# Expert stage: rows gathered by an indirect DMA and transposed, one-hot columns on ScalarE, job order alternated

## The reference, cut to what matters

```
g_sel = argmax(hf @ w_r1 + b_r1)              # one of 4 groups per token
top_p, top_i = top_k(softmax(e_logits of the group), 2)
expert_id = g_sel * 4 + top_i                 # 2 of 16 experts per token
combine = sum(one_hot(expert_id) * g_w * top_p)
hid = silu(hf @ w_gate[e]) * (hf @ w_up[e])   # width 256, per expert e
out = sum over e of (hid * combine[:, e]) @ w_down[e]
x = x + out
```

## Time and profile before

| | us |
|---|---|
| median of 3 runs | 1548.86 (1538.7 to 1549.76) |
| the profiled execution: time | 1550.05 |
| its span (first to last instruction) | 1547.3 |

### The profile page before, as it was taken

How to read it: one execution, slowest core, us unless ns; L and a number is a source line. 1 busy time by engine, 2 the same in 40 slices (tenths; PEclk the granted TensorE clock), 3 DMA queues, 4 the chain that set the end, 5 groups by cost and what they waited for, 6 DMA issues and landing times.

```text
span 1547.3 us, 18980 instructions
## 1 busy us (share of the span) xinstructions
PE 1440.7 (93%) x7049; PEld 1137.5 (74%) x7049; DVE 737.5 (48%) x1502; ACT 718.1 (46%) x1176; POOL 578.9 (37%) x261
## 2 busy tenths in 40 slices
PE   5999888989899998999899999999999888999998
PEld 4787665457777765867778777888887776888886
DVE  2196454444520224247854351233323376777775
ACT  4542325234642546445444755435322435555661
POOL 3265111003253311413322244223543156676762
PEclk9899999889999998999999999999999879999999
DMA  4232111003552211312222122212343036565552
GB/s 149 68 104 78 45 42 36 16 22 109 177 153 82 68 55 42 103 47 69 76 68 62 55 77 82 82 61 89 102 139 99 14 115 199 177 181 186 178 185 89
DMA packets 82003, 146.21 MB, mean 94 GB/s; under 512 B 12382, under 2 KB 14740, under 8 KB 81908
## 3 DMA queue, kind: packets, MB, share of 16 engines
q1 hardware_dynamic: 78288, 140.40, 29.5%
q10 hardware_dynamic: 3332, 4.53, 1.0%
q0 software_dynamic: 288, 0.02, 0.0%
HBM read 140.72 MB, written 4.19 MB: 94 GB/s over the span
## 4 chain that ended last, share of the span: by engine, by line
PE 76%; DVE 14%; ACT 6%; issue 2%; DMA 1%; POOL 0%; SPq 0%; DVEq 0%; ACTq 0%
PE ps L894 17%; PE ps L895 17%; PE ps L896 17%; PE ps L1349 4%; DVE perm L2664 3%; DVE work L2491 2%; PE ps L1421 2%; PE ps L1422 2%; DVE best L2489 2%; PE ps L1033 1%; PE ps L1234 1%; PE ps L1251 1%; PE ps L1207 1%; PE ps L1288 1%; PE ps L1269 1%
## 5 line engine op out<-in xcount | busy, mean ns | idle before, releaser
L841 POOL TENSOR_TENSOR w_lo<-raw,w_hi 128x1024 fp32r<-128x1024 f32 (+2 forms) x190 | 454.3, 2405 | 861.5 <-ACT w_hi L1599 832.5
L1599 ACT ACTIVATE w_hi<-raw 128x1024 fp32r<-128x1024 f32 (+3 forms) x206 | 208.7, 1038 | 121.1 <-PE ps L896 109.6
L894 PE MATMUL ps<-w_hi,act_hi 128*128 128x512 f32 (+1 forms) x560 | 231.7, 414 | 7.5 <-POOL w_lo L841 5.9
L895 PE MATMUL ps<-w_lo,act_hi 128*128 128x512 f32 (+1 forms) x560 | 219.6, 392 | 0.0
L896 PE MATMUL ps<-w_hi,act_lo 128*128 128x512 f32 (+1 forms) x560 | 219.1, 391 | 0.0
L894 PE MATMUL ps<-w_hi,mix_hi 128*128 128x512 f32 x384 | 161.7, 421 | 11.1 <-DVE mix_lo L2225 6.4
L896 PE MATMUL ps<-w_hi,mix_lo 128*128 128x512 f32 x384 | 152.2, 396 | 0.0
L895 PE MATMUL ps<-w_lo,mix_hi 128*128 128x512 f32 x384 | 152.2, 396 | 0.0
L894 PEld LDWEIGHTS ps<-w_hi,act_hi 128*128 128x128 f32 (+1 forms) x560 | 104.6, 187 | 47.8 <-issue 14.2
L896 PEld LDWEIGHTS ps<-w_hi,act_lo 128*128 128x128 f32 (+1 forms) x560 | 104.3, 186 | 25.1
L895 PEld LDWEIGHTS ps<-w_lo,act_hi 128*128 128x128 f32 (+1 forms) x560 | 104.7, 187 | 23.7 <-issue 1.7
(11 more groups left out here) (467 smaller groups left out, 2646.9 us busy)
## 6 DMA issues: line engine op xcount, KB each, us to landing
raw<-in_w_in SPq DMA_DIRECT2D x92, 512.0 KB, 3.6
raw<-in_w_gate SPq DMA_DIRECT2D x64, 256.0 KB, 2.9
raw<-in_w_up SPq DMA_DIRECT2D x64, 256.0 KB, 3.3
raw<-in_w_down SPq DMA_DIRECT2D x32, 512.0 KB, 4.1
raw<-in_w_out SPq DMA_DIRECT2D x16, 512.0 KB, 3.7
raw<-in_w_mem_kv SPq DMA_DIRECT2D x16, 512.0 KB, 4.6
raw<-in_w_o_gla SPq DMA_DIRECT2D x8, 512.0 KB, 3.8
raw<-in_w_o_dsa SPq DMA_DIRECT2D x8, 512.0 KB, 3.8
```

The costliest lines, as they stand in the source:

```text
L841: pool.tensor_tensor(lo[:, 0:a], raw_slot(g)[:, 0:a], hi[:, 0:a].bitcast(F32), ALU.subtract).then_inc(*POOL.done(("w_lo", g)))
L894: pe.matmul(dst, l_hi, r_hi, start=start, stop=False, skip_group_check=skip)
L895: pe.matmul(dst, l_hi, r_lo, start=False, stop=False, skip_group_check=skip)
L1599: nc.scalar.activation(split_slot(g)[0][:, 0:a], raw_slot(g)[:, 0:a], ACTF.Copy).then_inc(*ACT.done(("w_hi", g)))
```

## The change

- From pair 1 on the rows of a pair come by two indirect DMAs on GpSimd, each 128 rows of 4 KB, from x stored in `out` in device memory. SyncE stores x there ahead of the fifth expert unit (four stores of 512 KB, counted by `spilled`). The token numbers ride in `combine_r` as two more columns, so that `combine_s` (now 36 columns) yields them; VectorE copies them to `ids`.
- `row_turn` (`xturn`) transposes the gathered rows on TensorE, 4 chunks of 128 features a job, 4 jobs a pair; ScalarE and VectorE evict 128 columns at a time.
- `perm` of pairs 1 to 7 is made by ScalarE: Abs(iota - so), then Relu(1 - that). Pair 0 stays on VectorE.
- Four slots for `y_hi` and `y_lo`; unsort jobs of a pair are spread over the next even and odd visit, four each; the odd visit alternates them with the row jobs; `combine_s` and the gather stand at the end of even visits (visit 0: after `up`).
- VectorE loads the branch register after its part of `turn` in visit 3 (the fourth).

```diff
@@ make_order @@
         pair = e // 2
-        gather = [("resort", pair + 1, 0), ("resort", pair + 1, 1), ("combine_s", pair + 1), ("resort", pair + 1, 2), ("resort", pair + 1, 3)]
+        gather = [("combine_s", pair + 1), ("gather", pair + 1)] if pair + 1 < N_EXP // 2 else []
+        rows = [("xturn", pair + 1, j, i) for j in range(2) for i in range(2)]
         turns = [("permT", pair + 1, j) for j in range(2)]
-        if e < 2:
-            jobs = [gather, turns][e]
+        back = [("unsort", e - 2 - e % 2, 2, t, n) for t in ((2, 3) if e % 2 else (0, 1)) for n in range(2)] if e >= 2 else []
+        wanted = [("weights", E_UNITS * e + 9 + i) for i in range(4)]
+        order += [("up", e), wanted[0]]
+        if e % 2 == 0 and 2 <= e < N_EXP - 2:
+            order += [("perm", pair + 1, 2, 3)]
+        if e == 0:
+            order += gather + [wanted[1], ("turn", e), wanted[2], wanted[3]]
+        elif e % 2 == 0:
+            order += back[:2] + [wanted[1], ("turn", e)] + back[2:] + [wanted[2], wanted[3]]
         elif e == N_EXP - 1:
-            jobs = [("unsort", e - 1, 1, t, n) for n in range(2) for t in range(NT)]
-        elif e % 2:
-            jobs = gather + turns
+            one = [("unsort", e - 1, 1, t, n) for n in range(2) for t in range(NT)]
+            order += back + [wanted[1]] + one[:2] + [("turn", e), wanted[2], wanted[3]] + one[2:]
         else:
-            jobs = [("unsort", e - 2, 2, t, n) for t in range(NT) for n in range(2)]
-        at = (len(jobs) + 1) // 2
-        wanted = [("weights", E_UNITS * e + 9 + i) for i in range(4)]
-        order += [("up", e), wanted[0]] + jobs[:at - 1] + [wanted[1]] + jobs[at - 1:at] + [("turn", e), wanted[2]]
-        order += jobs[at:] + [wanted[3], ("down", e), ("weights", E_UNITS * e + 14)]
-        if e and e < N_EXP - 3:
-            order += [("perm", (e + 3) // 2, *((0, 1) if e % 2 else (2, 3)))]
+            order += back[:2] + rows[:1] + [wanted[1], ("turn", e)] + back[2:3] + rows[1:2] + back[3:] + [wanted[2]] + rows[2:3]
+            order += turns[:1] + rows[3:] + [wanted[3]] + turns[1:]
+        order += [("down", e)]
+        if e % 2 == 0 and e:
+            order += gather
+        order += [("weights", E_UNITS * e + 14)]
+        if e % 2 and e < N_EXP - 3:
+            order += [("perm", pair + 2, 0, 1)]
@@ tiles @@
-        y_hi = sb("y_hi", [P, 2, D], SC + 44, F32R)
-        y_lo = sb("y_lo", [P, 2, D], SC + 52, F32R)
+        y_hi = sb("y_hi", [P, 4, D], SC, F32R)
+        y_lo = sb("y_lo", [P, 4, D], SC + 44, F32R)
+        xg = sb("xg", [P, 2, 2, D], SC + 16)
@@ SyncE, at the loads of weights @@
+                if g == expert_unit + RAW_SLOTS:
+                    for t in range(NT):
+                        sp.wait_ge(*DVE.after("x", "w_out21", t))
+                        sp.dma_start(out[0, P * t:P * (t + 1), :], x1[:, t, :]).then_inc(spilled, 16)
@@ GpSimd @@
+                elif step == "gather":
+                    pair = a[0]
+                    pool.wait_ge(spilled, 16 * NT)
+                    pool.wait_ge(*DVE.after("ids", pair))
+                    if pair < 3:
+                        pool.wait_ge(*PE.after("resorted", 0, 3))
+                    else:
+                        pool.wait_ge(*PE.after("xturned", pair - 2, 1, 1))
+                    for j in range(2):
+                        pool.indirect_dma_start(xg[:, pair % 2, j, :], None, out[0, :, :],
+                                                bass.IndirectOffsetOnAxis(ids[:, pair % 2, j:j + 1], 0)).then_inc(g_in[pair % 2], 16)
@@ TensorE @@
+            def row_turn(pair, j, i):
+                bank = job_bank["xturn", pair, j, i]
+                claim(bank, (DVE, ("s_lo", 2 * pair + j, 4 * i + 3)))
+                pe.wait_ge(g_in[pair % 2], 32 * ((pair + 1) // 2))
+                for k in range(4):
+                    tr = pe.transpose(ps[:, bank, P * k:P * k + P], xg[:, pair % 2, j, paired_rows(4 * i + k)], ident[:, :])
+                tr.then_inc(*PE.done(("xturned", pair, j, i)))
@@ ScalarE @@
+            def one_hot(pair, *tiles):
+                if pair == 0:
+                    return
...
+                for t in tiles:
+                    for j in range(2):
+                        e = 2 * pair + j
+                        op = nc.scalar.activation(perm[:, t, P * j:P * j + P], iota[:, :], ACTF.Abs, bias=so_minus[:, t, e:e + 1])
+                    op.then_inc(*ACT.done(("perm_d", pair, t)))
+                act.wait_ge(*ACT.after("perm_d", pair, tiles[-1]))
+                for t in tiles:
+                    nc.scalar.activation(perm[:, t, :], perm[:, t, :].bitcast(F32), ACTF.Relu, bias=1.0,
+                                         scale=-1.0).then_inc(*ACT.done(("perm", pair, t)))
+            def row_turn(pair, j, i):
+                if pair >= 2:
+                    act.wait_ge(*PE.after("up", 2 * pair - 3))
...
+                for k in range(4 * i, 4 * i + 4):
+                    nc.scalar.activation(mix_hi[:, k, at:at + P], ps[:, job_bank["xturn", pair, j, i], P * (k % 4):P * (k % 4) + P], ACTF.Copy,
+                                         scale=gain_pairs[:, k:k + 1]).then_inc(*ACT.done(("s_hi", pair, j, k)))
             def down(e):
-                if e >= 2:
-                    act.wait_ge(*PE.after("spent", e - 2))
+                if e >= 4:
+                    act.wait_ge(*PE.after("spent", e - 4))
@@ VectorE @@
+                dve.wait_ge(tok_in, 16)
+                dve.tensor_copy(combine_r[:, :, 34:36], tokens[:, :].unsqueeze(2).to_broadcast([P, NT, 2])).then_inc(*DVE.done(("token_r",)))
             def one_hot(pair, *tiles):
                 if pair:
+                    return
...
+                dve.tensor_scalar(so_minus[:, :, :], so[:, :, :], -1.0, None, ALU.mult).then_inc(*DVE.done(("so_minus",)))
             def combine_sorted(pair):
+                if pair >= 3:
+                    dve.wait_ge(g_in[pair % 2], 32 * ((pair - 1) // 2))
+                dve.tensor_copy(ids[:, pair % 2, :].unsqueeze(2), both[:, :, 34:35]).then_inc(*DVE.done(("ids", pair)))
+            def row_turn(pair, j, i):
+                dve.wait_ge(*ACT.after("s_hi", pair, j, 4 * i + 3))
...
+                for k in range(4 * i, 4 * i + 4):
+                    low_part(("s_lo", 2 * pair + j, k), mix_lo[:, k, at:at + P],
+                             ps[:, job_bank["xturn", pair, j, i], P * (k % 4):P * (k % 4) + P], mix_hi[:, k, at:at + P],
+                             gain_pairs[:, k:k + 1])
             def overflow():
-                active = load_flags(dve, "dve")
+                elif step == "turn":
+                    turn(*a)
+                    if a[0] == 3:
+                        active = load_flags(dve, "dve")
```

More of the change, by code:

```diff
@@ L550, in program @@
         over_in = semaphore("over_in")
+        spilled = semaphore("spilled")
+        tok_in = semaphore("tok_in")
+        g_in = [semaphore(f"g_in{i}") for i in range(2)]
         const_in = semaphore("const_in")
@@ L561, in program @@
         stored = semaphore("stored")
-        jobs = [step for step in order if step[0] in ("combine_s", "resort", "permT", "unsort")]
+        jobs = [step for step in order if step[0] in ("combine_s", "resort", "xturn", "permT", "unsort")]
         job_bank = {step: (2, 3, 7)[i % 3] for i, step in enumerate(jobs)}
@@ L1382, in up @@
                 for k in range(KC):
-                    pe.wait_ge(*DVE.after("s_lo", pair, k))
+                    pe.wait_ge(*DVE.after("s_lo", e, k))
                     if k % 2 == 0:
@@ L1420, in unsort @@
                     cols = slice(512 * n, 512 * n + 512)
-                    pe.matmul(ps[:, bank, :], turned, y_hi[:, e % 2, cols], start=(e == e0), stop=False)
-                    mm = pe.matmul(ps[:, bank, :], turned, y_lo[:, e % 2, cols], start=False, stop=(e == e0 + count - 1))
+                    pe.matmul(ps[:, bank, :], turned, y_hi[:, e % 4, cols], start=(e == e0), stop=False)
+                    mm = pe.matmul(ps[:, bank, :], turned, y_lo[:, e % 4, cols], start=False, stop=(e == e0 + count - 1))
                 last = t == NT - 1 and n == 1
@@ L1571, in _ @@
                     perm_turn(*a)
+                elif step == "xturn":
+                    row_turn(*a)
                 elif step == "up":
@@ L1803, in overflow @@
                     ACT.section = "overflow"
+                    act.wait_ge(spilled, 16 * NT)
+                    act.wait_ge(*PE.after("down", N_EXP - 1, 1))
+                    for t in range(NT):
+                        act.dma_start(x_over[:, t, :], out[0, P * t:P * (t + 1), :]).then_inc(over_in, 16)
                     for k in range(KC):
```

72 lines of the change are left out of this document (43 added, 29 removed).

## The result

The changed kernel takes **1561.08 us** in the median of 5 runs (1554.3 to 1565.2), the kernel before 1546.77 in the same comparison. The ratio is 1.0097, with a 95% interval of 1.0055 to 1.0139: 0.6 to 1.4% slower, where 1527 us was forecast and the range ended at 1552. The profiled execution took 1554.3 us with a span of 1552.5.

The account below looks back on a forecast made before the run. TensorE was taken as the bound, busy 33.9 of a pair's 34.4 us. Savings of 7.5 + 11 + 3.2 + 2.4 - 2.2 = 22 us take 1550.05 us to 1528, as median 1527 us; range 1502 to 1552.

Parts of the forecast that it names:

- TensorE's work and the other engines' loads: Steady pair: 28.4 us without waits on TensorE, ScalarE 25, GpSimd 26.3, DMA engines about 73%, no table loads.
- The odd visit's bank chain: Odd visit: jobs sharing three banks wait for evictions; 10.65 us from first row job to down's end, 3.3 of it waits.
- G: Time of the odd visit's first row job, counted from the even visit's start; forecast 21.6 us, low end 20.3.
- the third rival: Odd visits: first row job waits for the gather, more if the clock halves; pair above 34.4 us, 1567 us; chance 0.11.
- 4 us to land: Gather's landing after GpSimd's 1.2 us each, taken nearest to the half-MB SyncE row of 4.1 us.
- high bound for landing: Gather taken to land in 7.0 us, as the stores of x did, giving a first row job at 27.0 us.
- rival (c): Odd visits: first row job waits for the gather, pair above 34.4 us; decides from G = 23.75; 1567 us; chance 0.11.
- rival (b): The gather takes what the sort gave: G from 23.5 to 25, pair 34.2 to 35.6 us, 1545 us; chance 0.19.
- The reason added to (c): GpSimd, writing the gather's descriptors, waits for a VectorE operation, at most 1.2 us per gather; G = 22.8 to 24.
- it moves nothing but G: Remainders-bound rival: GpSimd at 4 us a gather comes to 31.9 us, about the forecast's pair; no separate chance.
- Visits 0 to 2: First three expert visits: visit 2 without one-hot blocks before hid; 8.5 us saved, 7.5 with a margin for weights.
- Visits 14, 15 and the tail: Last visits: visits 13 and 14 save 3.2 us; the tail saves 2.4 without VectorE's idle at the register's load.

Follow-up runs that it names:

- e2_fixed_ids: Changed kernel with every gather taking pair 0's token numbers (wrong rows), issued at the start of the even visit; ratio to the kernel before 0.9918.
- e7_quarter: Changed kernel with each gather fetching 1 KB instead of 4 KB a row; 1549.04 us in one run.
- e11_fixed_late: Changed kernel with every gather taking pair 0's indices (wrong rows), the gather's place unchanged; ratio to the kernel before 1.0090.
- e10_between: Changed kernel with combine_s ahead of weight steps w2 and w3 and the gather between them, all rows right; ratio to the kernel before 1.0082.
- e6_direct: Changed kernel with each indirect gather replaced by a plain DMA of the same bytes from a fixed place; 1550.25 us in one run.
- e1_early: Changed kernel with combine_s and the gather ahead of weight steps w2 and w3 in even visits, real indices; ratio to the kernel before 1.0020.
- e12_fixed_early: Changed kernel with pair 0's indices for every gather (wrong rows), issued ahead of weight steps w2 and w3; ratio to the kernel before 1.0004.
- e4_reg: Kernel before with only the branch register's load moved to VectorE's visit 3; ratio to the kernel before 1.0021.
- e8_early_perm: Changed kernel with all four one-hot tiles made at the odd visit's end and the gather after the even visit's first two unsorts; ratio to the kernel before 0.9994.

## Why the prediction was wrong

**TensorE's work and the other engines' loads: right.** A pair without waits is 29.1 us in e2_fixed_ids (28.4 forecast), ScalarE 24.5 (25), GpSimd 25.9 (26.3), DMA 74% (73%). No table load came.

**The odd visit's bank chain: right but for 1.1 us.** From G to the next even visit it is 11.7 us in e2_fixed_ids and 11.6 in the changed kernel, 10.65 forecast. The forecast had VectorE done with the first four columns at G+2.95; it is done at G+3.7 in e2_fixed_ids, where ScalarE starts on them 1.4 us after G and not 0.45, behind a weight copy. At the lower clock the chain is hardly longer: 11.3 to 12.1 us over the changed kernel's six odd visits, 11.2 to 11.5 in e7_quarter at full clock. The 0.43 us matmuls mostly fill time in which TensorE would have waited for evictions, so the halved clock, which the third rival counted on, cost about half a us a pair.

**"When is G?": the step that failed.** Forecast 21.6 us into the even visit, measured 24.4 in the mean of six. The mis-sized term is "4 us to land", which from the start of the second gather is 5.2 us. In the four visits whose indices were in time that gather starts at 17.0 (16.4 forecast), and TensorE has the rows 6.5 to 8.1 us later; in the two with late indices it starts at 19.1 and the rows are there 5.4 and 5.7 later. The 4 us were taken from the row of half a MB on SyncE, the median of 32 loads of w_down. The forecast's own high bound for landing, 7.0 us from the stores of x, was the nearer row. e11_fixed_late and e10_between show that the late indices were not what made the pair long: with indices in time the rows still come at 23.3 to 25.3. e7_quarter shows that the rows' own bytes are a part of it, and e6_direct that the indirect form is not, but for GpSimd's 0.9 us. The rest goes out just when GpSimd's last remainders have released raw buffers, beside the loads that those release; how it divides between this traffic and a fixed delay was not tested and stays open. In the two visits shown G is late by 2.9 us and the chain longer by 1.0, about the 3.8 us by which the mean pair of 36.0 is above the forecast's 32.2.

By the Trainium skill's page "DMA: Bandwidth & Descriptors", section "Anatomy of one DMA — SWDGE (gpsimd) path", half a MB would take an estimated 3.2 us and a quarter of it 2.3; the trace doesn't agree: 4.7 to 8.0 us, and 3.3 to 5.3 for the quarter, with the DMA engines loaded.

**A pair at 36.0 is rival (c), at a lower price.** It was to decide from G = 23.75 for a pair; with the chain 1.1 us longer it decides from 22.7, and G was 24.4, as in rival (b). The reason added to (c), a gather that waits for a VectorE operation, did not act in the changed kernel, where no gather holds GpSimd longer than 1.05 us; it shows in e1_early and e12_fixed_early, with 1.8 to 1.9 us for the first gather of a pair. The rivals' mechanisms were there; the chance of 0.11 for (c) was too low because the bank chain was taken without a margin.

**A gather that hides is not free.** The forecast cost its GpSimd time as harmless because averages left room ("it moves nothing but G"). e1_early and e12_fixed_early show that 2.2 to 3.1 us ahead of a remainder come out at TensorE by way of a raw buffer, a load and ScalarE's order.

**Visits 0 to 2: 7.5 us forecast, 2.3 measured to silu 3.** Visit 2 did lose its 6.5 us wait (silu 2 to silu 3 is 13.0 us, 24.15 before), but visit 1, rows and all without unsorts to cover it, took 20.45 us where it had taken 10.89, at a clock of 0.67. TensorE's timeline has waits of 2.58 us for hid, 2.07, 0.86 and 0.84 us for mix_lo in it; the forecast let visit 1 end 2 us later than before. The gap it meant to save is not steady either: in e4_reg, whose code is the same there, the 6.5 us wait is 0.9, and silu 0 to silu 3 takes 44.8 us and not 52.0. Against that execution the changed kernel loses 4.9 us here. The forecast took a gap seen in one execution for a lasting one.

**Visits 14, 15 and the tail: a saving counted without its price.** Visit 14 is 3.6 us shorter, as forecast, which is the four unsort jobs (4 x 0.91) that moved out of it. They are now in visit 15, and the last additions wait for TensorE:

```profile
1544.53 4.87 DVE L2822 TENSOR_TENSOR x<-ps,x 128x512 f32<-128x512 f32 x8 [2.13 <-PE ps L1465]
```

The forecast set against them only a part of the 2.71 us of idle time, which it took for the register's load. e4_reg shows that moving the load doesn't remove that time (2.75 us), and its last stretch is no shorter: 20.7 us from silu 15 on, 20.5 before. The 2.2 us that the forecast charged visit 3 for the load didn't come either. In the sum these 2.4 us saved and 2.2 charged nearly cancel, by luck.

**The sum**, from silu 0 on, by the forecast's own cuts, forecast and measured: visits 0 to 2 -7.5 and -2.3; five pairs from visit 3, with the register's load, -8.8 and +9.1; visits 13 and 14 -3.2 and +0.8; from silu 15 on -2.4 and +2.7. Together -22 and +10.3. The five pairs make 18 of these 32 us.

## What to carry to other kernels

When a matmul is replaced by a transfer, cost the transfer at its place: count which loads are released just before it is issued, and take its landing from the slowest row of that size, not from the median of the most frequent one. Then follow the issuing engine's time through every buffer that its next work frees, since an engine that idles for nearly a third of its time can still be late for one buffer. And try the parts alone: here the small part, one-hot columns on ScalarE, was worth 0.4%, and the large one, 53.6 us of sorting matmuls for 12.2 of transposes, gave nothing in any order with real indices.

## What the runs showed of the hardware

- A gather of 128 rows by GpSimd holds it 0.96 us whether the rows have 4 KB or 1 KB, and 1.8 to 1.9 us where it comes up beside a weight remainder on VectorE (e1_early, e12_fixed_early); a plain DMA of the same bytes holds it 0.55.
- Half a MB gathered lands in 4.7 to 8.0 us beside weight loads, a quarter of it in 3.3 to 5.3. Its landing varied by 2 us at one and the same place (e10_between), and a start 2 us sooner brought the rows 0.2 and 1.4 us sooner (e11_fixed_late).
- A VectorE remainder with both inputs in SBUF takes 1.22 us alone and 3.35 beside the second of two of GpSimd's. In e8_early_perm it takes 8.15 beside three of them (7.10 us in all), about their time and its own: it lost to each in turn. It can also win between two: once it took 1.64, and GpSimd's two took 5.76 us, not 4.76. The Trainium skill's page "SBUF — State Buffer", section "Who interferes with whom", says that a VectorE operation with two inputs in SBUF contends with GpSimd's reads, and that the shared ports are held exclusively; the trace agrees, and adds that the one that waits can lose several times in a row.
- After waits of 3.2 to 4.9 us for rows TensorE went on at half its clock (0.43 us for 512 columns, not 0.23). Where evictions bound the stretch that cost about half a us in 11.3.
- VectorE idled for 2.7 us at a branch that was not taken, whether its register was loaded just ahead of it or twelve visits earlier (2.71 us in the kernel before, 2.75 in e4_reg).
